# Layer-norm pieces dealt out one per gate block and into the next sequence's first convolution block; gate by tile with both weight halves loaded

## The reference

```
proj = h @ w_in                         # u, c, b, z_a, q, k, v, z_b, g_a, g_b
y_a  = short_conv_branch(u, c, b, z_a)  @ w_proj_a
y_b  = diff_attention_branch(q, k, v, z_b) @ w_proj_b
merged = sigmoid(g_a) * y_a + sigmoid(g_b) * y_b
r = alpha * h + merged @ w_out
r = r + sigmoid(r @ w_ple_gate) * (p @ w_ple)
h = layer_norm(r, ln_g, ln_b)
```

## Time and profile before

| what | us |
|---|---|
| median of 3 runs | 5554.53 |
| lowest and highest run | 5550.63 and 5649.88 |
| the profiled execution, device time | 5548.78 |
| its span on the profiled core (the slowest, core 2) | 5547.4 |
| spans of the 8 cores | 5519.6 to 5547.4 |
| TensorE busy on that core | 5160.2 |

### The profile page before, as it was taken

How to read it: one execution, slowest core, us unless ns; L and a number is a source line. 1 busy time by engine, 2 the same in 40 slices (tenths; PEclk the granted TensorE clock), 3 DMA queues, 4 the chain that set the end, 5 groups by cost and what they waited for, 6 DMA issues and landing times.

```text
span 5547.4 us, 94905 instructions; the slowest of 8 cores (5519.6 to 5547.4 us)
## 1 busy us (share of the span) xinstructions
PE 5160.2 (93%) x35648; PEld 2897.2 (52%) x35648; DVE 2239.3 (40%) x3317; ACT 2983.4 (54%) x3998; POOL 385.6 (7%) x467
## 2 busy tenths in 40 slices
PE   7998999999899899999989989999998998999997
PEld 3445565644444566564434456656444445656643
DVE  2424333345442433334544243333464434333346
ACT  2326777834332687782433368678243236868723
POOL 1110000001111000001110100000111110000000
PEclk9999999999999999999999999999999999999998
DMA  7341110048334011004842400100583331010054
GB/s 82 31 42 15 13 13 9 5 82 151 61 31 46 10 13 13 9 5 84 149 68 27 43 13 9 13 9 5 100 155 46 31 39 14 7 13 9 21 83 118
DMA packets 448572, 233.79 MB, mean 42 GB/s; under 512 B 370208, under 2 KB 419616, under 8 KB 447616
## 3 DMA queue, kind: packets, MB, share of 16 engines
q0 software_dynamic: 420976, 156.20, 25.3%
q1 hardware_dynamic: 27152, 71.52, 3.7%
HBM read 350.31 MB, written 33.55 MB: 69 GB/s over the span
## 4 chain that ended last, share of the span: by engine, by line
PE 62%; ACT 22%; DVE 7%; issue 6%; DMA 2%; ACTq 0%; POOL 0%; DVEq 0%; SPq 0%; POOLq 0%
PE ps L113 53%; ACT reg L115 21%; PE ps L115 9%; DVE reg L115 6%; DMA reg<-xT 1%; ACT L115 1%; DMA wbuf<-w_in 1%; ACTq L93 0%; DVEq L93 0%; DMA out<-reg 0%; POOL wbuf L122 0%; DVE ybuf L115 0%; ACT ybuf L115 0%; POOL xbf L122 0%; DVE mabuf L115 0%
## 5 line engine op out<-in xcount | busy, mean ns | idle before, releaser
L115 ACT ACTIVATE reg<-ps 128x1024 bf16<-128x1024 f32 (+3 forms) x3168 | 2561.2, 840 | 2202.3 <-PE ps L115 1507.8
L113 PE MATMUL ps<-xbf,wbuf 128*128 128x512 bf16 x8064 | 1956.0, 383 | 140.6 <-DVE reg L115 57.4
L113 PE MATMUL ps<-reg 128*128 128x129 bf16 (+6 forms) x15360 | 1749.8, 245 | 168.6 <-ACT reg L115 127.8
L113 PEld LDWEIGHTS ps<-reg 128*128 128x128 bf16 (+1 forms) x15360 | 1134.5, 99 | 624.7 <-issue 252.1
L113 PEld LDWEIGHTS ps<-xbf,wbuf 128*128 128x128 bf16 x8064 | 790.1, 99 | 1098.4 <-issue 189.4
L115 PE MATMUL ps<-reg 128*128 128x512 bf16 (+1 forms) x3648 | 978.4, 281 | 0.0
L115 DVE TENSOR_TENSOR reg<-reg 128x512 f32<-128x512 f32 (+4 forms) x606 | 506.3, 836 | 374.4 <-ACT reg L115 312.2
L122 POOL DMA_DIRECT2D wbuf<-w_in x296 | 260.0, 893 | 4530.2 <-PE ps L115 4522.1
L115 DVE TENSOR_TENSOR reg<-ps,reg 128x512 f32<-128x512 f32 x384 | 262.6, 690 | 703.8 <-PE ps L115 558.9
L115 DVE COPY reg<-ps 128x387 f32<-128x387 f32 (+1 forms) x384 | 174.2, 509 | 874.6 <-PE ps L115 874.6
L115 PE MATMUL ps<-xbf,wbuf 128*128 128x512 bf16 x1152 | 440.7, 383 | 0.0
(11 more groups left out here) (62 smaller groups left out, 2618.5 us busy)
## 6 DMA issues: line engine op xcount, KB each, us to landing
wbuf<-w_in POOLq DMA_DIRECT2D x288, 256.0 KB, 5.7
reg<-xT SPq DMA_DIRECT2D x16, 2048.0 KB, 17.0
out<-reg SPq DMA_DIRECT2D x64, 512.0 KB, 4.5
wbuf<-w_out POOLq DMA_DIRECT2D x16, 1024.0 KB, 9.9
wbuf<-w_pg POOLq DMA_DIRECT2D x16, 1024.0 KB, 13.5
xbf<-xT POOLq DMA_DIRECT2D x24, 512.0 KB, 20.4
wbuf<-w_pa POOLq DMA_DIRECT2D x32, 256.0 KB, 5.5
wbuf<-w_in POOLq DMA_DIRECT2D x8, 1024.0 KB, 8.6
```

Source lines behind the costliest of these rows:

```text
L113: eng.prog.append(lambda f=f, a=a, kw=kw: f(*a, **kw))
L115: eng.prog.append(lambda f=f, a=a, kw=kw, s=sc.sem: f(*a, **kw).then_inc(s, 1))
```

## The change

There are four edits. The order of the gate blocks becomes tile by tile, with both weight halves taken at the start of the stage; `keep=1` makes the second `w_next` issue nothing, so that the first half's slot isn't refilled while it is in use. `queue_norm` puts an empty piece behind `stats`, so a tile has 10 pieces; `stage_wo` takes a piece after every second group instead of every group, and before each gate stage all pieces but one are taken. The list `back` outlives the sequence: what is left at its end is taken during the next sequence's first convolution block, three pieces after each of its four tiles. For that the convolution's buffers are laid out anew, `usb` first, then the set for even blocks, and the set for odd blocks only when block 1 begins.

```diff
+    def w_next(key, keep=0):
         i = wstate["next"]
-        while wstate["issued"] < min(len(plan), i + NW):
+        while wstate["issued"] < min(len(plan), i + NW - keep):
             w_issue(wstate["issued"])
             wstate["issued"] += 1
...
+    back = []
+    def behind():
+        if back:
+            fn = back.pop(0)
+            if fn is not None:
+                fn()
     def run_seq(s):
         region.reset()
-        bgb = [region.take((S,), F32) for _ in range(2)]
-        zsb_c = [region.take((S,), F32) for _ in range(2)]
-        tb = [region.take((S,), F32) for _ in range(2)]
-        hb = [region.take((S + 2,), F32) for _ in range(2)]
         usb = [region.take((512,), F32) for _ in range(2)]
...
+        def conv_set(k):
+            for vs, bs, nm in ((bgb, b_bg, "bg"), (zsb_c, b_zs, "zs"), (tb, b_t, "t")):
+                vs.append(region.take((S,), F32))
+                bs.append(region.claim(vs[-1], nm, NT))
+            hb.append(region.take((S + 2,), F32))
+            b_h.append(region.twins(hb[-1], "h", NT + 1))
             pr.op(dve, A(nc.vector.memset, hb[k][:, 0:1], 0.0), writes=(b_h[k][NT],))
             pr.op(dve, A(nc.vector.memset, hb[k][:, S + 1:S + 2], 0.0), writes=(b_h[k][NT],))
+        conv_set(0)
...
         for cc in range(8):
             k = cc % 2
+            if cc == 1:
+                while back:
+                    behind()
+                conv_set(1)
...
+                if cc == 0:
+                    for _ in range(3):
+                        behind()
...
         def stage_wo(pt):
...
-                        behind()
+                        if oc % 2 == 1:
+                            behind()
...
         def stage_gate(pt):
-            for g in range(2):
-                wf, wb = w_next(("pg", s, pt, g))
-                for tt in (pt, pt + 1):
+            w0 = w_next(("pg", s, pt, 0))
+            w1 = w_next(("pg", s, pt, 1), keep=1)
+            for tt in (pt, pt + 1):
+                for g, (wf, wb) in enumerate((w0, w1)):
                     for tb in range(4):
                         nxt = gate_block(wf, wb, tt, g, tb, k % 2)
...
-                    if g == 1:
-                        prev()
-                        prev = None
-                        if tt + 2 < NT:
-                            load_res(tt + 2)
-                            load_p(tt + 2)
-                        queue_norm(tt)
+                prev()
+                prev = None
+                if tt + 2 < NT:
+                    load_res(tt + 2)
+                    load_p(tt + 2)
+                queue_norm(tt)
...
             back.append(stats)
+            back.append(None)
...
             stage_wo(pt)
...
+            while len(back) > 1:
+                behind()
             stage_gate(pt)
-        while back:
-            behind()
+        if s + 1 == NSEQ:
+            while back:
+                behind()
```

More of the change, by code:

```diff
@@ L338, in w_issue @@
         pr.dma(pool, pairs, s_w[slot], reads=(), writes=(b_w[slot],))
-    def w_next(key):
+    def w_next(key, keep=0):
         i = wstate["next"]
         assert plan[i][0] == key, (plan[i][0], key)
-        while wstate["issued"] < min(len(plan), i + NW):
+        while wstate["issued"] < min(len(plan), i + NW - keep):
             w_issue(wstate["issued"])
@@ L347, in w_next, with wf @@
         slot = i % NW
-        return (lambda kc, c0, n: wbuf[:, slot, kc, c0:c0 + n]), b_w[slot]
+        def wf(kc, c0, n):
+            assert wstate["issued"] <= i + NW, ("slot taken", key)
+            return wbuf[:, slot, kc, c0:c0 + n]
+        return wf, b_w[slot]
     def mm_group(bank_i, lhs_fn, rhs_fn, nk, reads, rows=slice(0, 128), cols=slice(0, 512)):
@@ L394, in build @@
                   (wple_t[:, :, :], w_ple.rearrange("(c p) n -> p c n", p=128))], s_setup2, writes=(b_const2,))
+    back = []
[4 more added lines that the diff above has]
+                fn()
     def run_seq(s):
         region.reset()
-        bgb = [region.take((S,), F32) for _ in range(2)]
-        zsb_c = [region.take((S,), F32) for _ in range(2)]
-        tb = [region.take((S,), F32) for _ in range(2)]
-        hb = [region.take((S + 2,), F32) for _ in range(2)]
         usb = [region.take((512,), F32) for _ in range(2)]
[L403 to L406, removed]
         b_u = [region.claim(v, "u") for v in usb]
-        for k in range(2):
+        bgb, zsb_c, tb, hb, b_bg, b_zs, b_t, b_h = [], [], [], [], [], [], [], []
+        def conv_set(k):
[4 more added lines that the diff above has]
+            b_h.append(region.twins(hb[-1], "h", NT + 1))
             pr.op(dve, A(nc.vector.memset, hb[k][:, 0:1], 0.0), writes=(b_h[k][NT],))
             pr.op(dve, A(nc.vector.memset, hb[k][:, S + 1:S + 2], 0.0), writes=(b_h[k][NT],))
+        conv_set(0)
         def conv_tail(cc, ts):
@@ L761, in run_seq @@
         pr.dma(sp, [(gb[:, :, :], d_lngb)], s_gb, writes=(b_gb,))
-        back = []
         def load_res(tt):
@@ L773, in load_p @@
                    writes=(b_ptb[tt % 2],))
-        def behind():
-            if back:
-                back.pop(0)()
         def stage_wo(pt):
```

## The result

Four executions were timed: 5474.28, 5483.62, 5589.99 and 5858.31 us. The last two were disturbed (one die ran at a lower clock), so the median of all four, 5536.81, which lies outside the forecast's range, can't be set beside it, and every comparison from here on leaves such executions out. The other two stand against 5550.63 and 5554.53 of before. Their ratio is 0.9867, with an interval of 0.9825 to 0.991: some 74 us less, where the sum forecast 88.2. The change is within 2%, and the two times are inside the range of the prediction, 11 and 21 us above its value. The profiled execution took 5483.62 us; its slowest core is now core 0, not core 2.

The account below looks back on a forecast made before the run. TensorE was taken as the bound, so only its idle or low-clock stretches could give time: boundary 57.4, joins 25.7 (gate stages included) and end 5.1 sum to 88.2 us, 5548.78 to 5460.6, as a median 5463; range 5434 to 5498.

Parts of the forecast that it names:

- the boundary: Between sequences: all TensorE idle time (51.0 us) and the low clock after it (6.4) go, a gain of 57.4 us.
- The third rival: The boundary closes only in part: 1.5 us of cover is missed, three boundaries keep 45 us; 5506, chance 0.10.
- the end: Last sequence: 10 instead of 13 norm operations follow the gate and VectorE lags 1.2 us less; gain 5.1 us.
- the mechanism of the join: Between pairs: residual issued at E (first gate stage's end) + 6.8, gate 8.5 us after landing, `w_out` wait 6.5.
- the gain of the joins: Between the pairs: the gate begins 6.0 us earlier in the first join, 5.5 in the other three; 22.5 us.
- The rule that I had weighed against the change: In the join: DMA engines alternate between queues with work, so the moved `w_out` half slows the residual and whatever queues behind.
- The rival built on it: The DMA engines bound the join: `w_pg` lands at 1353.0, the joins give nothing; 5486, chance 0.18.
- The gate stages: Second gate stages: the low clock goes, 8.8 us gained; a 1.4 us wait at the fourth block costs 5.6.
- The hidden join: Residual takes 11.3 us, weights come in time, TensorE bounds the join; about 52 us gained there, 5431, chance 0.08.
- The slower rival: In the join TensorE awaits the moved `w_out` half; at 50 us to land, 5584; chance 0.04.

Follow-up runs that it names:

- The carry alone: Layout and carry of the change, with the output and gate stage order of the kernel before; 5502.36 and 5502.01 us, ratio to before 0.991.
- the last kernel: The version with the output stage tile by tile, with the second pair's gate stage by tiles too; 5443.19 and 5443.36 us, ratio to before 0.981.
- the kernels that go by tiles: Carry kept, second pair's output stage tile by tile: 5466.52 and 5463.85 us; also with the load first, 0.9866, or gate stage by tiles too, 0.981.
- the two repeats: The changed kernel run again without edit on two other chips: 5503.29 us on one, 5480.07 and 5482.59 us on the other.

## Why the prediction was right, and where it was not

**Right: the boundary.** 57.4 was forecast; 55.0 came on core 2, from whose rows it was worked out. Over the eight cores it was 42.4 to 55.6, in the mean 50.8; why core 0 gave only 44.6 is open. The working held to a few tenths: norm pieces end 29.0 after the gate (29), the convolution starts at 30.6 (30.5), the memset waits for no write, the first group takes 1.67. The carry alone shows it in time, 50 us. The third rival, cover missed, falls.

**Right: the end.** 5.4 against 5.1. In the step from the sum to a median, 5463 instead of 5460.6 takes about half of the 5.75 us that it names; all of it gives 5466, which changes nothing here.

**Right: the mechanism of the join.** The issue at E + 6.8 (6.8), the gate 8.3 to 9.4 after the landing (8.5), the wait for `w_out` in the middle of the output stage of 4.4 to 7.4 us (3 to 7), and a wait of 0.5 to 1.6 at the fourth gate block (1.4) all came on cores 0 and 2 as worked out.

**The step that failed: the gain of the joins, 22.5 us.** The step was: "if the load takes as long as before, the gate begins 6.0 us earlier". It did not take as long. In core 2's first join it took 22.1 against 21.9, and the gain was 5.9 us. In the other three it took 21.9, 22.7 and 21.9 where before had 17.2, 18.3 and 19.8, and they gained 1.1, 0.3 and 4.1 instead of 5.5 each. The four loads are longer by 11.2 us, and the joins gave 11.5 instead of 22.5. This is the whole shortfall of that term on that core. That the late weight half is the cause is shown by the run that moved it alone (20.9 to 22.6 on core 0, 4.0 more in the mean of 32 joins), and by the one that had the load go first (11.5 to 16.2, with the weights slower).

The DMA packets show how. In before, one `w_pg` half stood on GpSimd's queue beside the residual, and the next came 13 us later; in the change two loads were queued together. In core 0's second join (E is 2672.4 in before, 2669.8 in the change), from some 14 to some 18 us after E, the residual's queue (q1, SyncE's) had the engines to itself in before, since GpSimd's queue (q0) moved next to nothing between its two loads; in the change it got about half. Packets, MB and share of the 16 engines, before and then after:

```profile
q1 hardware_dynamic: 742, 1.63, 104.6%
...
q0 software_dynamic: 4, 0.00, 0.5%
...
q0 software_dynamic: 311, 0.32, 57.4%
q1 hardware_dynamic: 311, 0.63, 51.5%
```

Counted in steps of half a microsecond over the 32 joins, the residual had the engines to itself for 4.2 us in the mean in before, 0.1 in the change, and never in the run that moved the half alone. In before the six slowest loads (19.8 to 22.9 us) had 0.5 to 2.0 us of this and the six fastest (13.7 to 14.9) 5.0 to 7.0, so this pause also goes with much of the difference between the cores. Core 2's first join had almost none to lose, and so kept its gain.

The trace of before held a warning: the DMA share was 1.02 in core 0's join. But the share alone doesn't say that the engines are full, since it goes up to 1.15 in a gate stage of the last kernel; which queue has the engines, and when, says more.

The rule that I had weighed against the change thus applied, in part. The Trainium skill (DMA: Bandwidth & Descriptors, "Queues, rings and completion order") says that an engine takes turns between the queues that have work. The trace agrees: while both queues moved packets in the joins of the change, GpSimd's had 0.52 and SyncE's 0.54 of the engines' time in the mean. The rival built on it (5486) came within 3 us of the profiled 5483.62, but in part by luck: it has no gain at all in the joins, where core 0, now the slowest, lost 3.2 us; and on core 0 the time ahead of the first join grew by 10 us and the boundaries gave 13 less than forecast, which that rival has not. And what that rival forecast, a wait for `w_pg` at the gate, is not there; the residual itself was slowed.

**Mis-sized too: which core the sum was made on.** The joins were costed on core 2, the slowest, which had longer loads than most. Core 0's were 13.7 to 17.2 long and became 21.0 to 23.1, so its joins took 3.2 us more than before. Over all cores a join gained 0.6 us, that is 2.4 for an execution, and after the change the slowest core was one that had gained nothing there. By core, four joins gave from 14.2 us to a loss of 11.4. The gate stages came out at 1.9 on core 2 and 2.7 on core 0 where the net was 8.8 - 5.6 = 3.2.

The hidden join, the second rival, needed the residual in 11.3 us; it was reached by needing it later, beside fewer loads, in the kernels that go by tiles. The slower rival needed a `w_out` half of over 41 us; the longest in a join of any kernel here was 26.0.

What stays open: why the first `w_pg` half of before takes 12 us to land on some cores and 19 on others, which goes with the length of that pause, and why the times of the change spread from 5474 to 5503 over three measurements. In the execution of 5503 the last stretch from convolution to output took 1217 us on cores 4 and 5, against 1202 on the same cores in the first profile. The time ahead of the first join, which moved by up to 15 us from core to core, is part of the spread too; no run tested either.

## What to carry to other kernels

Before a load is moved into a stretch, read there, on several cores, which DMA queue moves packets when: here a pause between two loads of one queue was what kept a load on another short, and a load moved into it took that away (4.7 us in the mean of 32 joins). The sum has to use the longer times. Cost a term on all cores, not on the slowest alone; once it is removed there, the next core sets the time. Here an order of work that needs the load later, which also moved another load out of its way, gave 38 us more than the change; issuing the load earlier gave nothing in the joins.

## What the runs showed of the hardware

The same residual load of 2 MB took from 13.7 to 22.9 us over the cores and sequences of one execution of before, beside the same other loads; two weight loads queued together made this 20.5 to 24.2, and 18.2 to 24.0 in the two repeats. It moved its first packets 3.2 to 5.6 us after its issue in before, where GpSimd's queue already had the engines, and 1.0 to 3.1 after it where the load went first. A write of 512 KB that took 2.61 us at the boundary took 10.4 to 12.1 beside weight loads on another queue. And in the kernel with both stages by tiles, in joins without idle time, TensorE's granted clock was still 0.91 to 0.93, for a cost of 2.0 to 2.7 us, in 14 of 16 joins of cores 0 to 3 and in none of cores 4 to 7; in core 0's first join it was 1.00 for the first 12 us and then 0.81 for 14, with TensorE busy throughout.
